# First block's attention from the last tile to the first, with one projection moved between its units

## The reference, cut to what matters

```python
h = rms_norm(x, ln1_g[i]); z = h @ w_in[i]
m_out = mlstm(...)                     # the other mixer
# nsa, for every query position t and head
o_c = softmax(q @ Kc - slope * dist) @ Vc      # compressed keys: 31 blocks
o_s = softmax(q @ Ks - slope * dist) @ Vs      # "selected" keys, causal
o_w = softmax(q @ Kw - slope * dist) @ Vw      # sliding window, causal
a_out = g0 * o_c + g1 * o_s + g2 * o_w
x = x + concatenate([m_out, a_out]) @ w_out[i]
```

## Time and profile before

| | |
|---|---|
| median of 3 runs | 1600.36 us (1600.1 to 1601.32) |
| profiled execution | 1599.76 us |
| its span, first to last instruction | 1598.5 us |
| granted TensorE clock, mean | 0.993 of full |
| PE busy | 1539.1 us (96%) |
| DVE, ACT, POOL busy | 55%, 40%, 3% |
| stage nsa, first scores to the last fill | 202.3 to 324.5 us |

### The profile page before, as it was taken

One profiled execution on the slowest core, in us unless ns is written; L12 is line 12 of the kernel. 1 busy time (PEld: TensorE's weight loads), 2 busy tenths in 40 slices (PEclk: granted clock), 3 DMA queues, 4 the chain that ended last, 5 costly groups with the idle time before them and its releaser, 6 DMA issues.

```text
span 1598.5 us, 24516 instructions
## 1 busy us (share of the span) xinstructions
PE 1539.1 (96%) x10213; PEld 1314.8 (82%) x10213; DVE 879.5 (55%) x1589; ACT 637.3 (40%) x1134; POOL 48.8 (3%) x50
## 2 busy tenths in 40 slices
PE   7999989999999999999999899999999999999997
PEld 6888766678888888898988679999988987678886
DVE  4435566666635655966555555346665554555443
ACT  6242265543322334743444443223333343542333
POOL 0000001000000000020000000000110000000000
PEclk9999989999999999999999999999999999999999
DMA  7324100043233223431112102224431113013231
GB/s 256 106 57 106 53 14 15 27 131 106 82 103 106 84 100 104 95 80 54 53 54 57 51 27 67 93 80 146 80 80 54 54 54 77 17 40 118 80 119 53
DMA packets 166399, 125.13 MB, mean 78 GB/s; under 512 B 46608, under 2 KB 161296, under 8 KB 166288
## 3 DMA queue, kind: packets, MB, share of 16 engines
q1 hardware_dynamic: 166288, 123.56, 26.7%
HBM read 121.45 MB, written 2.10 MB: 77 GB/s over the span
## 4 chain that ended last, share of the span: by engine, by line
PE 85%; DVE 6%; ACT 5%; issue 2%; DMA 1%; SPq 1%; POOL 0%; DVEq 0%; ACTq 0%; POOLq 0%
PE bank L601 68%; PE bank L2779 2%; PE bank L2743 2%; PE bank L2759 2%; DVE w_lo L542 1%; PE bank L3159 1%; PE bank L2646 1%; PE bank L1566 1%; PE bank L1623 1%; ACT w_hi L533 1%; ACT probs L1496 1%; PE bank L3120 1%; PE bank L1442 1%; PE bank L3138 1%; DMA x_rows<-x 1%
## 5 line engine op out<-in xcount | busy, mean ns | idle before, releaser
L601 PE MATMUL bank<-h_hi,w_hi 128*128 128x512 f32 (+2 forms) x920 | 324.4, 372 | 13.0 <-DVE h_lo L791 7.9
L542 DVE TENSOR_TENSOR w_lo<-w_raw,w_hi 128x2048 fp32r<-128x2048 f32 (+2 forms) x116 | 238.8, 2058 | 167.6 <-ACT w_hi L533 167.0
L601 PE MATMUL bank<-h_hi,w_lo 128*128 128x512 f32 (+2 forms) x920 | 318.0, 366 | 0.0
L601 PE MATMUL bank<-h_lo,w_hi 128*128 128x512 f32 (+2 forms) x920 | 317.8, 365 | 0.0
L533 ACT ACTIVATE w_hi<-w_raw 128x2048 fp32r<-128x2048 f32 (+2 forms) x116 | 199.2, 1718 | 69.4 <-DMA w_raw<-w_in 29.9
L601 PEld LDWEIGHTS bank<-h_hi,w_hi 128*128 128x128 f32 (+1 forms) x920 | 165.7, 189 | 49.9 <-issue 19.0
L601 PEld LDWEIGHTS bank<-h_hi,w_lo 128*128 128x128 f32 (+1 forms) x920 | 165.7, 189 | 28.7
L601 PEld LDWEIGHTS bank<-h_lo,w_hi 128*128 128x128 f32 (+1 forms) x920 | 166.0, 189 | 27.0 <-issue 0.5
L601 PE MATMUL bank<-g_hi,w_hi 128*128 128x264 f32 (+1 forms) x752 | 181.2, 307 | 1.5 <-DVE z_a L2175 0.9
L601 PE MATMUL bank<-g_hi,w_lo 128*128 128x264 f32 (+1 forms) x752 | 178.7, 303 | 0.0
L601 PE MATMUL bank<-g_lo,w_hi 128*128 128x264 f32 (+1 forms) x752 | 178.6, 303 | 0.0
(11 more groups left out here) (594 smaller groups left out, 2580.2 us busy)
## 6 DMA issues: line engine op xcount, KB each, us to landing
w_raw<-w_in SPq DMA_DIRECT2D x44, 1024.0 KB, 5.3
w_raw<-w_up SPq DMA_DIRECT2D x32, 512.0 KB, 4.9
w_raw<-w_in SPq DMA_DIRECT2D x40, 256.0 KB, 4.4
w_raw<-w_down SPq DMA_DIRECT2D x8, 1024.0 KB, 4.9
w_raw<-w_out SPq DMA_DIRECT2D x8, 1024.0 KB, 5.0
w_raw<-w_out SPq DMA_DIRECT2D x8, 512.0 KB, 3.5
w_raw<-w_ple_gate SPq DMA_DIRECT2D x4, 1024.0 KB, 5.0
w_raw<-w_o_attn SPq DMA_DIRECT2D x8, 512.0 KB, 3.4
```

Of the source, the lines that this page charges most:

```text
L542: DV.e.tensor_tensor(wlo[u % RING][:, 0:n], raw[u % RING][:, 0:n], whi[u % RING][:, 0:n].bitcast(F32), ALU.subtract).then_inc(*w_low(u))
L601: ins = PE.e.matmul(out, stationary[a](k), moving[b](k)[i], start=first and n == 0, stop=last and n == 2)
```

## The change

The units run from tile 3 to tile 0, and all order that hangs on it (which buffer was used before, whose `a_lo` DVE makes, the numbers of the branches) is turned with them. The n = 1 part of the projections leaves the mlstm stage and becomes the first three fill steps of the attention stage, on all of PE, ACT and DVE, so there are 15 fill steps. Their places are written out in `fill_at`: fill k is given in step `fill_at[k]`, the fifteenth after the last unit. Steps 1 to 3 hold the projection of the sliding branch, 4 to 7 the m features, the others residual products. Units of the sliding branch wait for its keys and values. `v_features` moves to memory of its own, and the wait for the compress matmul ahead of its first use goes; `a_hi` and `a_lo` wait until the projection's row factors in the memory beneath them are no longer read. Unit 0's factors are copied in unit 1's turn instead of in its own.

```diff
@@ placement
-        WT, c = place("mlstm_weights", [P, 2, TT, S], F32, c)
+        WT, weights_end = place("mlstm_weights", [P, 2, TT, S], F32, c)
...
-        vT, _ = place("v_features", [P, S], F32, work_at)
...
+        c = max(c, weights_end)
         for n in range(2):
             n_factor[n], c = place(f"branch_factor{n}", [P, 4, P], F32, c)
+        vT, c = place("v_features", [P, S], F32, c)
@@ pe_rest_steps
-            for n in range(2):
-                w = pe_unit()
...
+            yield from pe_branch_steps(0, dense_1, compress)
+
+        def pe_branch_steps(n, dense, before=()):
+            w = pe_unit()
+            b = pe_bank(dense, "ksw", n)
+            pe_features(H1, KT, w, [columns(0)], S, [b]).then_inc(*product("ksw", n))
+            yield
+            drain(before)
+            b = pe_bank(dense, "vsw", n)
+            pe_features(H1, KT, w, [columns(P)], S, [b]).then_inc(*product("vsw", n))
+            unit_end[w[2]] = ("vsw", n)
+            yield
+            b = pe_bank(dense, "vs", n)
+            PE.wait_ge(*evac.at("vsw", n))
+            for t in range(TT):
+                ins = PE.e.transpose(bank[:, b, t * P:(t + 1) * P], vT[:, t * P:(t + 1) * P], ident[:, :])
+            ins.then_inc(*v_turned(n))
+            yield
...
+        def ac_branch_steps(n, before=()):
+            yield
+            drain(before)
+            ac_split()
+            yield
+            AC.wait_ge(*v_turned.at(n))
+            AC.e.activation(vs[:, n, :, :].rearrange("p t c -> p (t c)"), bank[:, bank_of["vs", n], :],
+                            ACT.Copy).then_inc(*evac_a("vs", n))
+            yield
...
-                if n == 0:
-                    DV.wait_ge(*cmp_made.at(1))
-                else:
-                    DV.wait_ge(*v_turned.at(n - 1))
...
+        def dv_branch_steps(n, before=()):
+            dv_scaled(halves(kvT[:, 2 + n, :]), halves(bank[:, bank_of["ksw", n], 0:S]), row_1, ("ksw", n))
+            yield
+            drain(before)
+            dv_split()
+            if n:
+                DV.wait_ge(*v_turned.at(n - 1))
+            dv_scaled(halves(vT[:, :]), halves(bank[:, bank_of["vsw", n], 0:S]), row_1, ("vsw", n))
+            yield
+            yield
@@ the attention stage
-        units_n = [u for t in range(TT) for u in [(t, 0, 0)] + ...]
+        units_n = [u for t in reversed(range(TT)) for u in [(t, 0, 0)] + ...]
-        dense_n, dense_6 = ring(*[0] * 11, 6), ring(0, 1, 2, 3, 4, 5)
+        fill_at = (1, 2, 3, 4, 5, 6, 7, 11, 14, 17, 19, 21, 23, 25)
+        dense_n, dense_6 = ring(*[0] * len(fill_at), 6), ring(0, 1, 2, 3, 4, 5)
+        def filled_by(step):
+            return sum(at <= step for at in fill_at)
...
+                if br == 2:
+                    PE.wait_ge(*evac.at("ksw", 1))
...
-            if i > 1 and is_last(units_n[i - 1]):
+            if i and is_last(units_n[i - 1]):
                 ac_nsa_factors(units_n[i - 1])
...
             if i == 0:
                 ac_nsa_wide(unit)
-                ac_nsa_factors(unit)
...
+            if br == 2:
+                PE.wait_ge(*evac.at("vs", 1))
...
         def pe_mlstm_out_steps():
+            yield from pe_branch_steps(1, dense_n)
...
-                while given < 11 * min(step, len(units_n)) // len(units_n):
+                while given < filled_by(min(step, len(units_n))):
...
-            ac_a_high(TT - 1)
+            ac_a_high(0)
...
-            for t in range(TT - 1):
+            for t in reversed(range(1, TT)):
                 a_low(PO, t).then_inc(*h_low_p("a", t))
```

More of the change, by code:

```diff
@@ L730, in first_steps, with filled @@
                 yield next(steps)
-        def filled(items, fill, total, *stages_, apart=False):
+        def filled(items, fill, total, *stages_, apart=False, upto=None):
             given = [0]
@@ L736, in give @@
                 n = items.index(item) + 1
-                while given[0] < total * n // len(items):
+                while given[0] < (upto(n) if upto else total * n // len(items)):
                     next(fill, None)
@@ L1341, in ac_rest_steps @@
             yield from rest_order(compress, [ac_splits(aq_keys(a)) for a in range(2)])
[L1342 to L1351, removed]
+            yield from ac_branch_steps(0, compress)
+        def ac_branch_steps(n, before=()):
[7 more added lines that the diff above has]
+            yield
         def dv_rest_steps():
@@ L1363, in dv_rest_steps @@
                                              for a in range(2)])
[L1364 to L1370, removed]
-                    DV.wait_ge(*cmp_made.at(1))
-                else:
-                    DV.wait_ge(*v_turned.at(n - 1))
-                dv_scaled(halves(vT[:, :]), halves(bank[:, bank_of["vsw", n], 0:S]), row_1, ("vsw", n))
-                yield
-                yield
+            yield from dv_branch_steps(0, compress)
+        def dv_branch_steps(n, before=()):
[8 more added lines that the diff above has]
+            yield
         def mlstm_with(steps, rest):
@@ L1500, in pe_nsa_factors @@
             t, br, j0 = unit
-            wide = n_wide[(3 * t + br) % 2]
+            wide = n_wide[branch_number(t, br) % 2]
             PE.wait_ge(*n_flip.at(number_n[unit], 0))
@@ L1509, in ac_nsa_wide @@
             t, br, j0 = unit
-            n = 3 * t + br
+            n = branch_number(t, br)
             if n > 1:
-                AC.wait_ge(*product.at("n factors", *divmod(n - 2, 3)))
+                AC.wait_ge(*product.at("n factors", *branch_at(n - 2)))
             AC.wait_ge(*n_stat.at(t, br, "gated"))
@@ L1519, in ac_nsa_factors @@
             t, br, j0 = unit
-            n = 3 * t + br
+            n = branch_number(t, br)
             if n > 1:
-                AC.wait_ge(*n_out.at(*divmod(n - 2, 3), "out"))
+                AC.wait_ge(*n_out.at(*branch_at(n - 2), "out"))
             AC.wait_ge(*product.at("n factors", t, br))
@@ L1531, in dv_nsa_inverse @@
                 DV.wait_ge(*exp_of(unit))
-            if t > 1:
-                DV.wait_ge(*n_factor_made.at(t - 2, br, "wide"))
+            if t < TT - 2:
+                DV.wait_ge(*n_factor_made.at(t + 2, br, "wide"))
             DV.e.reciprocal(nstat[:, 4 + t % 2, br, :], nstat[:, 2 + t % 2, br, :]).then_inc(*n_stat(t, br, "inverse"))
@@ L1608, in pe_nsa_value @@
             t, br, j0 = unit
-            i, o = number_n[unit], 3 * t + br
+            i, o = number_n[unit], branch_number(t, br)
             pt = pt_s[i % 2]
@@ L1642, in dv_nsa_value @@
             DV.wait_ge(*n_valued.at(i))
-            if br == 2 or br and t:
-                DV.wait_ge(*n_out.at(*((t, 1) if br == 2 else (t - 1, 2)), "added"))
+            if br == 2 or br and t < TT - 1:
+                DV.wait_ge(*n_out.at(*((t, 1) if br == 2 else (t + 1, 2)), "added"))
             total, of_branch = a_sum[:, :, t * P:(t + 1) * P], part[:, :].rearrange("p (j q) -> p j q", j=4)
@@ L1661, in ac_mlstm_out_steps @@
         def ac_mlstm_out_steps():
+            yield from ac_branch_steps(1)
             for k in range(4):
@@ L1672, in dv_mlstm_out_steps @@
         def dv_mlstm_out_steps():
+            yield from dv_branch_steps(1)
             for k in range(4):
@@ L1691, in pe_nsa @@
             fill = pe_mlstm_out_steps()
-            filled(units_n, first_steps(fill, 11), 11, pe_nsa_score, pe_nsa_turn, pe_nsa_value, apart=True)
+            filled(units_n, first_steps(fill, len(fill_at)), 0, pe_nsa_score, pe_nsa_turn, pe_nsa_value, apart=True, upto=filled_by)
             for t, br, j0 in units_n[-2:]:
@@ L1738, in pe_mix_out @@
             PE.wait_ge(*n_flip.at(len(units_n) - 1, 1))
-            PE.wait_ge(*n_factor_made.at(TT - 1, 2, "features"))
-            PE.wait_ge(*n_out.at(TT - 1, 2, "out"))
+            PE.wait_ge(*n_factor_made.at(0, 2, "features"))
+            PE.wait_ge(*n_out.at(0, 2, "out"))
             drain(pe_residual_steps(dense_6, "ln2", A_in, 4, S))
```

34 lines of the change are left out of this document (13 added, 21 removed).

## The result

| | before | after |
|---|---|---|
| median | 1600.1 us | 1611.35 us (5 runs, 1605.33 to 1611.75) |
| ratio, 95% interval | | 1.0054 [1.0043, 1.0065]: slower |
| profiled execution, its clock | 1599.76 us, 0.993 | 1607.15 us, 0.992 |
| span | 1598.5 us | 1605.9 us |
| values' transposes of n = 0 to the output projection | 186.88 to 324.54: 137.66 us | 186.29 to 330.37: 144.08 us |

The forecast was 1602.6 us in a range of 1596.0 to 1606.0. The time is outside it: 9 us (by the ratio) to 11 us (by the medians) were lost where 2 were expected. The output projection starts at 330.37, past the 329 that was named as the limit. Two things are to be told apart: the profiled execution lost 7.4 us, and most other executions lose some 4 more, at a lower mean clock (0.988 or 0.989 in the three of 1611 and over, 0.992 and 0.993 in the other two).

What follows compares the result with a forecast made beforehand. TensorE was taken as the bound, losing 19.2 us of a 137 us stretch to idling and low clock. Its losses after summed to 21.45, ending the stage 2.2 us later: 1602.6 us, range 1596.0 to 1606.0.

Steps and rivals of the forecast that it cites:

- 1 fence: At the start of the attention, PE idles 3.3 us until DVE's last gate product is done.
- 3 values' transposes: In unit step 3, PE waits 4.2 us for DVE's values evacuation, queued behind the w_lo split.
- 4 m features: In unit steps 4 to 7, PE waits 1.6 us for ACT's copies out of the fills' shared PSUM bank.
- 5 factors, tiles 3 to 1: At branch ends in these tiles, seven PE waits for ACT's factor copy, 2.8 us together.
- 5 passage to tile 2: Going from tile 3 to tile 2, no fill covers DVE's softmax of the compressed unit: 0.7 us.
- 6 end: In tile 0, now last with a single fill in its wide units, PE waits 5.0 us for ACT.
- 2, 3, 6 low clock: Half-clock stretches after the starting wait, the values' transposes wait and the late wait: 1.35, 1.2 and 1.3 us lost.
- step 3 wait short: Rival, 22%: ACT's exps and split finish before PE needs the values, or tail waits overlap; 1597.2 us.
- the clock stays up: Rival, 15%: only the start of the attention runs at low clock; 2.5 us less than forecast, 1600.1 us.
- The gain: In the first tiles' thin start, low stretches at 212 and 232 us go, saving 5.1 us, and thin-start waits go.
- The slower rival: Rival, 25%: second low stretch after the values' transposes wait, and low clock reaching the output projection; 1606.0 us.
- 48 dense matmuls that cover nothing: Projection matmuls ahead of the attention's thin start, 12.5 us of the chain, taken as the prize to be hidden.

Runs made afterwards that it cites:

- the run with the evacuation first: Changed kernel with DVE evacuating the sliding branch's values ahead of the w_lo split instead of behind it; 1605.59 us, ratio 1.0031.
- the order alone: Changed kernel with the n = 1 projection back in the mlstm stage and eleven fills spread evenly, tiles still reversed; 1597.28 us, ratio 0.9984 to before.
- the busy fence: Changed kernel with 13 unused matmuls added on TensorE ahead of the wait for the gate products, other waits left idle; 1607.85 us, ratio 1.0045.
- the kept-busy kernel: Changed kernel with 38 unused matmuls added in three TensorE waits: gate products, values' transposes and late factor; 1602.19 us, ratio 1.0018.

## Why the prediction failed, by its steps

The measured loss of PE from the end of the first values' transposes (186.9) to the output projection is 143.5 - 117.8 = 25.7 us, against 21.45 forecast and 19.2 before. Waits as the brackets show them, low clock counted where PE works:

| step | forecast, us | measured, us |
|---|---|---|
| 1 fence | 3.3 | 3.47 |
| 3 values' transposes | 4.2 | 3.99 |
| 4 m features | 1.6 | 1.62 (0.50 + 0.20 + 0.72 + 0.20) |
| 5 factors, tiles 3 to 1 | 2.8 | 4.24 (seven waits, 3.19, one of them 1.32; and an extra one of 1.05) |
| 5 passage to tile 2 | 0.7 | 0.71 |
| 6 end | 5.0 | 4.23 (1.01 + 2.76 + 0.27 + 0.19) |
| what 19 waits cost beyond their brackets, 0.1 each, an estimate | 0 | 1.9 |
| 2, 3, 6 low clock | 1.35 + 1.2 + 1.3 | 2.45 + 1.35 + 1.75 |

These rows sum to 25.7. The 0.1 for each wait is the prediction's estimate and no run isolates it. It isn't needed for the comparison: left out on both sides, before loses 10.6 in brackets and 6.8 in low clock, after 18.3 and 5.55, and the difference of 6.4 us is the measured one (143.45 - 137.03).

**Right: the order of events and nearly every wait.** The three main ones came at the named instructions, from the named releasers, within 0.25 us; their sum is 18.3 us against 17.6. The rival "step 3 wait short" fell with the row at 213.04, and the cause named in step 3 is shown by the run with the evacuation first. The rival "the clock stays up" fell with the stretches at 212.4 and 321.6. In that sum there is some luck: step 5 was too small by 1.4 and step 6 too large by 0.8. The 1.6 of step 4 came out, but no run gave the fills banks of their own, so it isn't shown that the bank is their cause. The gain was named at the right place, the thin start, and the order alone does win 0.2%; of low clock, though, it wins 1.7 us and not the 5.1 of the sum, since its trace has two new low stretches of 3.4 us (at 202.7 and 305.1) for the 10.2 at 212 and 232.

**Failed, the bookkeeping (1.9 us).** The loss before, 19.2, had 0.1 us for each of 16 waits in it; the sum for after had none for its 19. The two were not made in the same way. Made alike, the forecast's own terms give 2.2 + 1.6 = 3.8 us for the stage, and not 2.2; the other 0.3 are three waits more.

**Failed, step 5 (1.4 us).** The splits of the fills at steps 14 and 19 stand in ACT's and DVE's queues ahead of the copies that PE wants. The step had a price for a factor wait and didn't walk through these queues as step 3 did. ACT of the kernel after, where the split stands ahead of the flip:

```profile
263.03 0.61 ACT L1528 ACTIVATE branch_inverse<-softmax_stats 128x512 f32<-128x512 f32 x1
263.55 1.04 ACT L534 ACTIVATE w_hi<-w_raw 128x1024 fp32r<-128x1024 f32 x1
264.49 0.47 ACT L1601 ACTIVATE probsT<-bank 128x384 f32<-128x384 f32 x1
```

and DVE behind it, where the low split stands ahead of the scores and its half of the flip:

```profile
264.72 1.22 DVE L543 TENSOR_TENSOR w_lo<-w_raw,w_hi 128x1024 fp32r<-128x1024 f32 x1 [1.78 <-ACT w_hi L534]
265.86 0.55 DVE L1476 CUSTOM_DVE_ANT_0 scores<-bank,distance 128x384 f32<-128x384 f32 x1
```

The run with these two fills a step later shows that the waits are theirs, and that a step later is no better place; that it is their splits is read from these rows. The 1.32 stands in the trace of the order alone as well, so it comes with the order and its fill at step 19 and not with the moved projection. The kernel before had the sign of it. The step read its factor waits as "between 0.3 and 0.7 elsewhere", but the earlier trace rows has one of 1.31 and the trace two more, of 1.12 and 0.86. At each of the three ACT does a fill's work ahead of the factor copy; at the 1.31 (kernel before):

```profile
228.08 0.66 ACT L645 ACTIVATE m_features<-bank,params 128x512 f32<-128x512 f32 x1
228.78 0.63 ACT L1668 ACTIVATE h_hi<-m_features 128x512 fp32r<-128x512 f32 x1
229.31 0.58 ACT L1524 ACTIVATE branch_factor<-bank 128x512 f32<-128x512 f32 x1
```

**Failed, steps 2, 3 and 6: the clock, the largest miss (1.7 us in this stage, 1.5 behind it, and 3.6 between this execution and the median).** The three terms of low clock were put at 3.85 us together and measured 5.55. The price of a low stretch was taken from the row at 188 as 3.4 us at half speed, with PE idle or thin for part of it. The first one was 6.8 us long, and one came at 355 us, in dense work 25 us after the stage, behind a wait that before has too. With the 1.9, the 0.7 that the waits exceed their sum, and 0.6 off because the seam came earlier, that makes the profiled execution 5.1 us longer than its forecast of 1602.0. The largest part is not in that trace at all: most executions of the changed kernel run at a clock of 0.987 to 0.990, and the trace of the busy fence at 0.988 shows one long execution, with the stretch at step 3 at 13.7 us, the last at 6.8, and two more far behind. Added up, some 6.8 of the 8.8 us between 1602.6 and 1611.35 are put down to the clock. The slower rival (25%, 1606.0) named this mechanism, a second low stretch behind a thin step 3 and more at the end; it was decided by a wait over 3 us in step 3, which I had put at 4.2 in the forecast itself. So the forecast contained the condition of the rival that should have replaced it, and the rival was sized for one execution and not for the median. In the changed kernel's own two traces the rival's two stretches are not there (3.4 us at step 3, and the clock is back at 1.00 before the output projection); only the trace of the busy fence has the first. Before's runs spread less (1599.0 to 1603.6 in 25 runs), so its own 0.6 us between profile and median said nothing of it.

**The balance of the change.** The order alone saves 2.7 us of the stage. The move, with its places of fills, then makes waits of 3.5, 4.0 and 1.6 us to cover 2.9 us of idle time, adds one wait at a split (1.05 for 0.37), and low clock comes with the long ones. "48 dense matmuls that cover nothing" was the prize as I read it from the kernel before; after the order is reversed the start is no longer thin, and there is little left to cover.

**Open.** Why the same wait goes with 3.4 us of low clock in one execution and with 13.7 in another; and in which stretches the long executions of the changed kernel itself are low, since none of them was profiled. How the cost of the move divides between the projection and the places of the other fills. That the remaining difference of the kept-busy kernel to the order alone (some 5 us) is all waits is argued from its stage (140.67 against 134.98), not tried piece by piece.

## What to carry to other kernels

Price a long wait of TensorE with the low clock that may follow it: here three waits, 10.2 us together, carried 6 to 8 us of low clock with them, seen in the medians more than in one trace. One profile does not size it: look at the mean clock of all runs. When work is moved between engines' hand-written steps, walk every instruction through each queue that it joins, at all its places and not only at the first; and where a change has two parts, price each against the other's result, since here the second wanted to cover what the first had already removed.

## What was not expected of the hardware

The length of a low stretch varies from execution to execution around the same wait: 3.4 us (the changed kernel, twice) or 13.7 (with the fence's wait filled) at the 4.0 us wait, 3.4 or 6.8 at the end. Whether there is one varies too: behind the same 1.86 us wait after the stage, seven of 14 profiled executions have one and seven none. Five executions of one kernel spread over 6 us (1605.33 to 1611.75), in line with their clocks (0.993 to 0.988). The Trainium skill, "TensorE: Matmul & The Clock Gate", Part 1, says of the start of a kernel that the count of matmuls at the lower clock differs from run to run; here low clock differs between executions in mid-kernel too. TensorE's matmuls without use, 38 of them and some 9 us long, made a kernel 6 to 8 us faster.
